# Down stage of a diffusion-transformer step: low parts by VectorE alone, another order of pairs, evictions and final sums

## What is computed

```python
def conv_ffn(h, w_up, w_conv, b_conv, w_down):
    u = h @ w_up                                   # (640, 1024) @ (1024, 5632)
    ...                                            # depthwise conv of width 3, bias
    a, g = jnp.split(u, 2, axis=-1)
    return (a * jax.nn.silu(g)) @ w_down           # (640, 2816) @ (2816, 1024)

    x = x + gt2 * conv_ffn(h2, w_up, w_conv, b_conv, w_down)
```

## Time and profile before

| | us |
|---|---|
| median of 3 runs | 966.84 (966.77 to 967.43) |
| the profiled execution's own time | 964.7 |
| its span, first to last instruction | 962.9 |
| TensorE busy in the span | 941.1 (98%) |
| VectorE busy | 687.1 (71%) |
| ScalarE busy | 483.1 (50%) |
| GpSimd busy | 474.6 (49%) |

### The profile page before, as it was taken

How to read it: one execution, slowest core, us unless ns; L and a number is a source line. 1 busy time by engine, 2 the same in 40 slices (tenths; PEclk the granted TensorE clock), 3 DMA queues, 4 the chain that set the end, 5 groups by cost and what they waited for, 6 DMA issues and landing times.

```text
span 962.9 us, 19064 instructions
## 1 busy us (share of the span) xinstructions
PE 941.1 (98%) x7447; PEld 854.1 (89%) x7447; DVE 687.1 (71%) x1241; ACT 483.1 (50%) x760; POOL 474.6 (49%) x362
## 2 busy tenths in 40 slices
PE   6999999999999999999999999999999999999996
PEld 5799899977788899999987999999999999778785
DVE  6508359962675769534946998777777778999977
ACT  5244165523765565341414375665555556566550
POOL 1375733223332316772723468999998886000112
PEclk9999999999999999999999999999999999999999
DMA  9897221226001123788651203688876232446792
GB/s 336 275 151 102 75 80 48 66 72 187 28 23 45 45 68 119 233 255 298 246 175 44 88 20 125 169 214 219 214 211 168 88 88 95 169 175 200 227 283 77
DMA packets 135683, 139.66 MB, mean 145 GB/s; under 512 B 9030, under 2 KB 105259, under 8 KB 135339
## 3 DMA queue, kind: packets, MB, share of 16 engines
q1 hardware_dynamic: 127592, 125.50, 41.4%
q0 software_dynamic: 6128, 11.64, 7.8%
q10 hardware_dynamic: 1875, 1.32, 0.4%
HBM read 127.14 MB, written 10.24 MB: 143 GB/s over the span
## 4 chain that ended last, share of the span: by engine, by line
PE 74%; DVE 12%; issue 4%; DMA 3%; SPq 3%; ACT 2%; POOL 1%; DVEq 0%; ACTq 0%; POOLq 0%
PE PA L1818 7%; PE PA L1820 6%; PE PA L1819 6%; PE PJ L1094 6%; PE PJ L1099 5%; PE PJ L1095 5%; DMA d_raw<-in_w_down_dram 2%; DVE d_far L3387 2%; PE PJ L1612 2%; SPq L607 2%; PE PA L1538 2%; PE PJ L1613 2%; PE PJ L1617 2%; PE PJ L1818 2%; PE PJ L1820 2%
## 5 line engine op out<-in xcount | busy, mean ns | idle before, releaser
L865 POOL TENSOR_TENSOR wlo<-wraw,whi 128x1024 fp32r<-128x1024 f32 x32 | 80.6, 2522 | 167.1 <-ACT whi L1954 166.8
L1094 PE MATMUL PJ<-h_hi,whi 128*128 128x320 f32 x336 | 104.8, 320 | 0.1
L1095 PE MATMUL PJ<-h_lo,whi 128*128 128x320 f32 x336 | 101.1, 309 | 0.0
L1954 ACT ACTIVATE whi<-wraw 128x1024 fp32r<-128x1024 f32 x39 | 41.0, 1052 | 71.0 <-PE PJ L1258 22.4
L1099 PE MATMUL PJ<-h_hi,wlo 128*128 128x320 f32 x336 | 76.5, 309 | 0.0
L1094 PEld LDWEIGHTS PJ<-h_hi,whi 128*128 128x128 f32 x336 | 63.0, 188 | 5.8 <-issue 3.6
L1032 POOL TENSOR_TENSOR behind<-behind_val,behind 128x512 fp32r<-128x512 f32 x40 | 60.1, 1503 | 10.2 <-ACT behind L2449 10.2
L1068 POOL DMA_DIRECT2D d_near<-ahead_dram x10 | 8.6, 864 | 112.8 <-ACT d_near L2486 112.8
L1095 PEld LDWEIGHTS PJ<-h_lo,whi 128*128 128x128 f32 x336 | 63.1, 188 | 0.0
L2478 ACT ACTIVATE d_hi<-d_raw 128x1024 fp32r<-128x1024 f32 x44 | 45.2, 1051 | 32.6 <-DMA d_raw<-in_w_down_dram 25.0
L1820 PE MATMUL PA<-h_hi,behind 128*128 128x320 f32 x192 | 59.3, 309 | 0.0
(11 more groups left out here) (637 smaller groups left out, 3357.5 us busy)
## 6 DMA issues: line engine op xcount, KB each, us to landing
wraw<-in_w_in_dram SPq DMA_DIRECT2D x72, 256.0 KB, 3.1
d_raw<-in_w_down_dram SPq DMA_DIRECT2D x33, 512.0 KB, 4.3
ada_rest<-in_w_ada_dram SPq DMA_DIRECT2D x32, 512.0 KB, 6.1
wraw<-in_w_up_dram SPq DMA_DIRECT2D x48, 256.0 KB, 4.5
raw_even<-in_w_up_dram SPq DMA_DIRECT2D x40, 256.0 KB, 4.4
ada<-in_w_ada_dram SPq DMA_DIRECT2D x16, 512.0 KB, 7.4
d_ahead<-in_w_down_dram SPq DMA_DIRECT2D x11, 512.0 KB, 4.6
d_ahead<-in_w_down_dram POOLq DMA_DIRECT2D x11, 512.0 KB, 5.8
```

The source lines that it names most:

```text
L865: pool.tensor_tensor(wlo[:, slot, 0:k, :], wraw[:, slot, 0:k, :], whi[:, slot, 0:k, :].bitcast(F32), ALU.subtract).then_inc(lo_done, done)
L1094: pe.matmul(out, whi[:, slot, w0 + k, :], hi(k)[:, tok], start=start and k == k0, stop=False)
L1095: pe.matmul(out, whi[:, slot, w0 + k, :], lo(k)[:, tok], start=False, stop=False)
L1954: act.activation(whi[:, slot, :, :], wraw[:, slot, :, :], ACT.Copy).then_inc(hi_done, done)
```

## The change

It makes seven edits, all behind the up stage.

- The ten adding DMAs of POOL and ACT's ten negatives before them are gone. DVE makes the low of units 0 and 1 in one subtraction of 128x1024 for every pair.
- DVE's six evictions between the halves stand ahead of the low of the token sums and of the far low of pair 1.
- On DVE and ACT the last pair (10) is taken up ahead of pairs 8 and 9 with its sums and its far low. Its near low and the low of its token sums come at the end (`PART_ORDER`, `SUM_ORDER`).
- PE's order of matmuls and SP's order of loads stay.
- In the final sums the gate times `u` (the part of tile 3 that is known before P4) is added to `x2` ahead of P4 (steps `p1`, `q1`), so that only P4 times the gate and one add are left for that tile (`m1`, `y1`).
- The adds of the far half of tiles 2 and 3 (`x0`, `x1`) and the last add of tile 2 (`y0`) go from DVE to POOL, which has seven adds there instead of four.
- SP's last stores wait for POOL's counter where POOL now does the add.

```diff
-TAIL = ["U0", "U1", "V0", "w0", "V1", "w1", "t0", "z0", "x0", "t1", "z1", "x1", "s0", "m0", "y0", "s1", "m1", "y1"]
+TAIL = ["U0", "U1", "V0", "w0", "V1", "w1", "t0", "z0", "t1", "z1", "p1", "q1", "s0", "m0", "m1", "y1"]
...
-PART_ORDER += [("early", KH - 1)] + [(name, k) for k in range(KH) for name in ("near", "sums", "far")]
+PART_ORDER += [("early", KH - 1)] + [(name, k) for k in range(KH - 3) for name in ("near", "sums", "far")]
+PART_ORDER += [("far", KH - 1)] + [(name, k) for k in (KH - 3, KH - 2) for name in ("near", "sums", "far")] + [("near", KH - 1), ("sums", KH - 1)]
+SUM_ORDER = list(range(KH - 3)) + [KH - 1, KH - 3, KH - 2]
...
             for i in range(2):
-                sp.wait_ge(y_set, tail_at(f"x{i}"))
+                sp.wait_ge(pooled_set, P_DOWN + 4 + i + 1)
                 y_out(2 + i, 1)
-            for i in range(2):
-                sp.wait_ge(y_set, tail_at(f"y{i}"))
-                y_out(2 + i, 0)
+            sp.wait_ge(pooled_set, P_DOWN + 7)
+            y_out(2, 0)
+            sp.wait_ge(y_set, tail_at("y1"))
+            y_out(3, 0)
...
-            for n in range(N_OPENED, N_DOWN - 1):
-                landing_low(n)
...
+            for i in range(2):
+                pool.wait_ge(y_set, tail_at(f"z{i}"))
+                x_ = x2[:, 2 + i, BANK:D]
+                pool.wait_ge(pooled_set, P_DOWN + 2 * i + 2)
+                pool.tensor_tensor(x_, x_, d_raw[0][:, 2 + i, :], ALU.add).then_inc(pooled_set, 1)
+            pool.wait_ge(y_set, tail_at("m0"))
+            x_ = x2[:, 2, 0:BANK]
+            pool.tensor_tensor(x_, x_, down_diag[:, 0, :, :].rearrange("p a n -> p (a n)"), ALU.add).then_inc(pooled_set, 1)
...
-                if name == "P7" and k < KH - 1:
-                    pe.wait_ge(low_landed[n % W_SETS], landed_low(n))
-                else:
-                    pe.wait_ge(actlo_set, PART_LOW["near" if name in ("P5", "P7") else "far", k])
+                pe.wait_ge(actlo_set, PART_LOW["near" if name in ("P5", "P7") else "far", k])
...
-            def down_negative(n):
-
-                out, units = (d_far[d_set(n)][:, :, :], slice(2, 4)) if n < KH else (d_near[d_set(n)][:, 1:2, :], slice(1, 2))
-                act.wait_ge(hi_done, weight_high(n, 2 if n < KH else 1))
...
-            for k in range(2, KH):
-                first_half(KH + k)
+            for k in SUM_ORDER[2:]:
+                down_high(KH + k, 0)
                 sums_high(k)
                 down_high(KH + k, 1)
...
-                units = slice(0, 1) if KH <= n < N_DOWN - 1 else slice(0, 2)
-                dve.tensor_tensor(d_near[d_set(n)][:, units, :], raw_of(n)[:, units, :], d_hi[d_set(n)][:, units, :].bitcast(F32),
+                dve.tensor_tensor(d_near[d_set(n)][:, :, :], raw_of(n)[:, 0:2, :], d_hi[d_set(n)][:, 0:2, :].bitcast(F32),
                                   ALU.subtract).then_inc(actlo_set, 1)
...
             weight_low(KH + 1)
-            sums_low(1)
-            far_low_units(KH + 1)
             dve.wait_ge(gates_in, 32)
...
+            sums_low(1)
+            far_low_units(KH + 1)
...
-            for k in range(2, KH):
+            for k in SUM_ORDER[2:]:
                 weight_sums(k)
-                weight_low(KH + k)
-                sums_low(k)
+                if k < KH - 1:
+                    weight_low(KH + k)
+                    sums_low(k)
                 far_low_units(KH + k)
...
+            weight_low(N_DOWN - 1)
+            sums_low(KH - 1)
```

More of the change, by code:

```diff
@@ L811, in down_rows @@
                     sp.wait_ge(hi_done, weight_high(n - 2, 2))
-                    sp.wait_ge(actlo_set, PART_LOW["opened" if 1 <= n - 2 < N_OPENED else "weight", n - 2])
+                    sp.wait_ge(actlo_set, PART_LOW["opened" if n > 2 else "weight", n - 2])
                     if n == 2:
@@ L1057, in _ @@
                 unit_low(c + 1, "S4")
[L1059 to L1064, removed]
-                else:
-                    pool.wait_ge(hi_done, weight_high(n, 2))
-                    out, rows = d_low(n, 1), ahead_dram[k, :, 1, :]
-                pool.dma_start(out, rows, accum_op=ALU.add).then_inc(low_landed[n % W_SETS], 16)
             pool.wait_ge(lo_done, L_DOWN)
@@ L3546, in _ @@
                 ps = product_at("P7", i)
-                dve.tensor_tensor(as_rows(u3_[:, i, :]), kept(0, i), as_rows(ps), ALU.add).then_inc(y_set, 1)
-                dve.wait_ge(y_set, tail_at(f"t{i}"))
-                dve.tensor_tensor(ps, ps, g_far, ALU.mult).then_inc(y_set, 1)
-                x_ = x2[:, 2 + i, BANK:D]
-                dve.wait_ge(pooled_set, P_DOWN + 2 * i + 2)
-                dve.wait_ge(y_set, tail_at(f"z{i}"))
-                dve.tensor_tensor(x_, x_, ps, ALU.add).then_inc(y_set, 1)
-            for i in range(2):
-                ps = product_at("P4", i)
-                dve.wait_ge(y_set, tail_at(f"t{i}"))
-                dve.tensor_tensor(ps, ps, u3_[:, i, :], ALU.add).then_inc(y_set, 1)
-                dve.wait_ge(y_set, tail_at(f"s{i}"))
-                dve.tensor_tensor(m_[:, i, :], ps, g_near, ALU.mult).then_inc(y_set, 1)
-                dve.wait_ge(y_set, tail_at(f"m{i}"))
-                x_ = x2[:, 2 + i, 0:BANK]
-                dve.tensor_tensor(x_, x_, m_[:, i, :], ALU.add).then_inc(y_set, 1)
+                dve.tensor_tensor(as_rows(u_[i]), kept(0, i), as_rows(ps), ALU.add).then_inc(y_set, 1)
+                dve.tensor_tensor(z_[:, i, :], ps, g_far, ALU.mult).then_inc(y_set, 1)
+            x_ = x2[:, 3, 0:BANK]
+            dve.wait_ge(y_set, tail_at("t1"))
+            dve.tensor_tensor(u_[1], u_[1], g_near, ALU.mult).then_inc(y_set, 1)
+            dve.wait_ge(y_set, tail_at("p1"))
+            dve.tensor_tensor(x_, x_, u_[1], ALU.add).then_inc(y_set, 1)
+            ps = product_at("P4", 0)
+            dve.wait_ge(y_set, tail_at("t0"))
+            dve.tensor_tensor(ps, ps, u_[0], ALU.add).then_inc(y_set, 1)
+            dve.wait_ge(y_set, tail_at("s0"))
+            dve.tensor_tensor(m_, ps, g_near, ALU.mult).then_inc(y_set, 1)
+            ps = product_at("P4", 1)
+            dve.tensor_tensor(ps, ps, g_near, ALU.mult).then_inc(y_set, 1)
+            dve.wait_ge(y_set, tail_at("m1"))
+            dve.tensor_tensor(x_, x_, ps, ALU.add).then_inc(y_set, 1)
 _INS = ["x_prompt", "x_sample", "c", "cache_na_k", "cache_na_v", "state_gla_fwd", "state_gla_bwd", "c_ctx", "w_ada",
```

36 lines of the change are left out of this document (11 added, 25 removed).

## The result

The changed kernel takes 959.98 us (median of six, 959.61 to 960.48), the kernel before beside it 967.03 (median of six): ratio 0.9932, 95% interval 0.992 to 0.9945. That is faster, by more than forecast: 962.7 was predicted, with 961.7 as the lower end of its range.

The account below looks back on a forecast made before the run. PE, 98% busy, was taken to hang at its end on DVE's far low of pair 10. 4.05 - 0.3 + 0.35 = 4.1 us off the median 966.84 gave 962.7 us, range 961.7 to 965.3.

Parts of the forecast that it names:

- The chain of DVE: DVE's operations in the down stage, rebuilt from the profile's rows: the last far low, pair 9's, ends at 938.67.
- Last pair ahead: Pair 10 before 8 and 9 on DVE: two P6 products follow PE's wait; last matmul at 953.6, 4.05 us earlier.
- Loads: Loads of the down stage land in 4.5 us without adding transfers, pair 7's in 5.2: 0.3 us of waiting subtracted.
- Evictions: DVE's evictions ahead of pair 1's lows: PE's first hole goes, pair 1 starts 2.12 us earlier, but this is hidden.
- The end: Final sums and stores behind PE's last matmul: 0.75 us less, 0.4 lost to stores running together, 0.35 kept.
- The rule against the row: Skill's rule: engines of slow GpSimd-queue DMAs often idle, so removing transfers gives loads nothing; rows' 31.7% share speaks against it.
- The first rival: Loads stay as they were, 6.2 us each: DVE waits 1.3 us, gain 3.1, time 963.7; chance 0.26.
- The step that failed: Last step of the sum: the profiled execution's 2.1 us under the median carried over, 966.84 - 4.1 = 962.7.
- The slower rival: Down stage's load loop takes over: gain used up at 7.05 us per load, 972.6 at 8.5; chance 0.06.

Follow-up runs that it names:

- the second run with adding transfers: Changed kernel plus ten adding transfers of 256 KB on POOL's queue into bytes nobody reads, run again beside plain ones: 963.49 us, ratio 0.997.
- another run with adding ones: Changed kernel plus ten adding transfers of 256 KB on POOL's queue into bytes nobody reads, first time: 963.47 us, ratio 0.9974.

## Why the prediction was wrong

- **The chain of DVE: right.** The last far low ends at 937.12 + 1.22 = 938.34, predicted 938.67. The 0.33 come from upstream, since the near low of pair 1 started at 889.45 and not at 889.81. The wait of 1.2 us for ACT at pair 10 is there (1.13).
- **Last pair ahead: right between the two profiled executions** (last matmul 953.26 for 953.6, or 953.9 with the wait for loads). Its value to DVE was underrated: undoing it put 1.78 us of waits for loads in the place of 1.13 for ACT, which the prediction never set against each other.
- **Loads: mechanism right, size off.** They land in 4.8 us, in the middle of the 4.5 and 5.2 taken, and DVE waited for none of them. The 0.3 us subtracted were not lost.
- **Evictions: right for PE**, whose 2.1 us were hidden. They cost DVE nothing in the sum, but undoing them lost it 0.5 us. **The end:** 0.35 predicted, 0.41 between the traces; the medians don't show it.
- **The rule against the row: the row decides.** By the rule of the Trainium skill (SBUF — State Buffer, section "SBUF: two separate sides") the transfers' engines would have been idle. The prediction left out the rule's condition, that a VectorE operation holds the port that it shares with GpSimd; whether one did, no run here shows. The adding transfers held 19.0% of the engines' time, plain ones of the same size 8.3%, and the loads went from 6.3 to 5.4 us. The first rival fell with it.
- **The step that failed** is the last one of the sum: "That execution lies 2.1 us under the median of the three runs, and I carry the difference over". The sum had 960.6 for the profiled execution (959.88 measured). From span to span it was 0.7 us short (0.36 upstream, 0.3 for loads, 0.06 at the end). The other 2.0 us are the carried difference, and it belonged to the kernel before, not to the machine. In 64 of 101 executions that kernel's clock was down, and their median is 1.78 us higher. In the one that was profiled, 1.34 us of this stand behind the hole of 2.5 us. The changed kernel's clock, with a hole of 1.10 us, fell in none of twelve executions. The prediction started from an execution in which the clock had stayed at 1.00, and did not ask why the other three took 2.1 us longer. So a shorter hole was worth its length and, on top, the clock behind it. That a fall behind this hole costs 1.6 us, and that filling the hole keeps the clock, is shown by experiment in the changed kernel with its hole made longer. For the kernel before it rests on the two traces and the 101 executions, since filling its hole gave nothing that could be measured.
- **The slower rival** (the load loop takes over at 7.05 us and more) did not come: the loads of pairs 3 to 9 landed in 4.1 to 5.4 us. Pair 10's own, which is not in that loop, took 6.6.

Put together, 4.8 us between executions with their clock and 1.5 us for the clock (966.18 over all 101 less 964.72) give 6.3. The measured gains were 7.0 and 5.5 us, each beside its own executions of the kernel before, whose median went from 965.8 to 967.0 between the sets; nothing here explains that scatter.

Open is what decides, in one execution, whether the clock falls. The executions profiled with a fall had last holes of 2.53, 2.54, 2.53, 2.54 and 2.90 us, those without one 2.53 and 2.23. The hole that went before does not decide either. In the second run with adding transfers, whose clock fell, the two holes are these:

```profile
936.33 0.50 PE L1838 MATMUL PA<-d_hi,e_hi 128*128 128x512 f32 x1 [0.42 <-DVE d_far L3369]
...
940.53 0.50 PE L1838 MATMUL PA<-d_hi,e_hi 128*128 128x512 f32 x1 [2.54 <-DVE d_far L3369]
```

They are nearly those of the earlier trace rows (0.46 and 2.53), where the clock stayed, and the kernel before with lows by DVE alone had no such first hole and lost its clock.

## What to carry to other kernels

Before costing an edit, hold the profiled execution's time against the median; where they differ by more than the scatter, find the stretch that makes the difference, and ask whether the edit removes its cause, before carrying it over. A hole of PE of the size seen here (2.5 to 2.9 us) costs its length and may cost over half as much again in the clock behind it (1.3 to 1.6 us), so shortening it, or filling it with work already at hand (the products of another pair, where their operands are there), pays more than the timeline shows. Transfers that add are no free arithmetic where loads are close to the path: compare them with plain ones of the same size.

## What the runs showed of the hardware

- In the five executions profiled with a fall, PE's granted clock stood, behind a hole of 2.5 to 2.9 us, at 0.50 (1.2 GHz) for some three windows of 1 us, and the matmuls that followed took 1.34 us longer in one execution, 1.6 in the others. With holes of 2.23 and 2.53 us it also stayed at 1.00, once each. In each profiled execution whose mean over the span was 0.999 or more there was no such stretch behind the last hole.
- A 256 KB transfer from POOL's queue that adds takes 2.3 times the engines' time of one that copies (19.0% and 8.3% of the stretch for 2.1 MB), and 512 KB loads beside it land 0.9 us later than beside plain ones (6.3 and 5.4 us; 6.9 in another run with adding ones).
